# First expert's rows: tiles 0 and 1 fetched back from memory, the other six gathered by 0/1 products

## The chip, the cores and the metric

The kernel runs on one core of a Trainium2 chip. The time is device microseconds of one execution; before the change the median of three runs is 958.38 us (955.35 to 960.75). The engines are PE (TensorE: PE the products, PEld the weight loads), DVE (VectorE), ACT (ScalarE), POOL (GpSimd) and SP (SyncE, which only issues DMAs here).

## The reference

One decoder layer over 1024 positions of width 1024, in f32: a hybrid token mixer, a cross-attention into 256 memory tokens, and a mixture of 16 experts of which each token takes 2. The part that matters:

```python
xa = memory_cross_attention(x, mem, xa_wq[l], xa_wk[l], xa_wv[l], xa_wo[l])
x = layer_norm(DEEPNORM_ALPHA * x + xa, ln_xa_g[l], ln_xa_b[l])
ffn = grouped_moe(x, router_w, router_bias, expert_w_gate[l], expert_w_up[l], expert_w_down[l])
x = layer_norm(DEEPNORM_ALPHA * x + ffn, ln_moe_g[l], ln_moe_b[l])
```

`grouped_moe` takes the router's logits of x, a sigmoid, the best of 4 groups, the best 2 experts of it, and sums the two experts' outputs by weight.

## The kernel before, in words

The program is a row of blocks (`project`, `prepare`, `attend`, `cross_attend`, `experts`, `overflow`). In a block each engine has its own instruction list, written out by hand in the order in which it runs; semaphores join the lists. At the end of a block all engines meet at a barrier. The change lies wholly in `cross_attend`.

Positions stand in 8 tiles of 128. `cross_attend` walks over the tiles (t = 0 to 7) in one software pipeline. For a tile, PE makes queries, scores, values and output products (`outputs`, into the accumulator `x_acc`). DVE adds the residual and takes the statistics (`residual`), POOL turns the variance into 1/sigma (`ln_rs`, L1788 and L1789), DVE normalizes (`norm`, which signals `x2_made`). PE transposes the normalized tile (`turn_x2`, into `x_tps`), ACT copies it out (`copy_x2`, L1535), PE multiplies it with the router's weights (`logits`, L1414), ACT takes the exponential (`neg_exp`, L1539).

Slots are given out in three batches: tiles 0 to 3, 4 and 5, 6 and 7. Per batch DVE ranks the experts (`rank_experts`) and chooses two (`choose`, which makes `selected_b`); PE counts, with 0/1 products against a triangle and ones, how many tokens before have the same expert (`place`, L1426 and L1429); DVE makes of the counts the number of each token's row in a table (`number`, L1665 to L1678), of which every expert has 176 rows ("slots").

A token's row then goes two ways.

* To memory: POOL scatters it with two indirect DMAs per tile (`scatter`, L1770) into `slot_rows` in HBM, zeroed long before. When all 16 scatters have landed, SP in the next block loads 176 rows for each expert (`x_rows`).
* To the first expert alone, without memory: `number` also makes a 0/1 matrix per tile (`in_first_expert`, 128 tokens x 176 slots, L1671), and `first_rows` (L1456) multiplies each 128-column slice of the tile with it. Eight such products of 176 columns per tile add up over the 8 tiles in four PSUM banks (`first_ps`); ACT copies the four to `xgT` (L1586), the transposed input of the first expert. `first_rows` of tile 0 opens the accumulation.

The block's end is thus: `logits` of tile 7, ACT's exponential, DVE's `rank_experts(2)` and `choose(2)`, PE's `place(2)`, DVE's `number(2)`, then side by side PE's last `first_rows` and ACT's copies, and POOL's scatters of tiles 6 and 7; then the barrier, and `experts` begins with the first expert's gate and up products (L2016).

POOL's list in the last steps is: 1/sigma of tile 6, the two scatters of tile 0, 1/sigma of tile 7, the scatters of tiles 1 to 7.

Of the kernel before, what the change touches and what calls it, by code (L numbers as in the profile page):

```python
# [15 lines left out]
P = 128  # L16
S, D = 1024, 1024
NT = S // P
KD = D // P
# [1212 lines left out]
def cross_attend(nc, k):  # L1232
# [70 lines left out]
    dve_chain, pool_chain = k.sem("chain6"), k.sem("pool_chain6")  # L1303
    flat = "p j c -> p (j c)"
    BATCHES = [(0, 4), (4, 6), (6, 8)]
    with nc.psum_tensor("x_tps", [P, 2, 512], f32) as tps, nc.psum_tensor("x_qps", [P, 512], f32) as qps, \
            nc.psum_tensor("x_sps", [P, 2, 512], f32) as sps, nc.psum_tensor("x_ops", [P, 512], f32) as ops, \
            nc.psum_tensor("x_acc", [P, 2, 512], f32) as acc, nc.Block(no_gpsimd_drain=True) as block:
# [4 lines left out]
        @block.sync  # L1313
        def _(sp):
            sp.wait_ge(q_lo, KD)
            for s in range(XH):
                sp.dma_start(rawo[:, s, :], A["xa_wo"][s * P:(s + 1) * P, :]).then_inc(o_loaded, 16)
            sp.dma_start(rw[:], A["router_w"].rearrange("(s p) e -> p s e", p=P)).then_inc(rw_loaded, 16)
            sp.dma_start(rb[:], over(A["router_bias"], [P, NE])).then_inc(loaded, 16)
            sp.wait_ge(v_sum, 2)  # L1320
            sp.dma_start(g[:], over(A["ln_xa_g"], [P, D])).then_inc(loaded, 16)
            sp.dma_start(b[:], over(A["ln_xa_b"], [P, D])).then_inc(loaded, 16)

            sp.wait_ge(w_lo, XH)
            sp.dma_start(paired(k.e_dn[:]), A["w_dn"][0].rearrange("s p n -> p s n")).then_inc(k.dn_loaded, 16)
            sp.dma_start(k.g3[:], over(A["ln_moe_g"], [P, D])).then_inc(k.gains_loaded, 16)
            sp.dma_start(k.b3[:], over(A["ln_moe_b"], [P, D])).then_inc(k.gains_loaded, 16)
            sp.wait_ge(q_sum, NT)
            for e in range(2):
                sp.dma_start(paired(k.e_gu[:, e]), A["w_gu"][e].rearrange("s p n -> p s n")).then_inc(k.gu_loaded[e], 16)  # L1330

        @block.tensor
        def _(pe):
# [99 lines left out]
            def outputs(t, heads=range(XH)):  # L1433
                pe.wait_ge(o_lo, t + 1)
                if t == 0:
                    pe.wait_ge(w_lo, XH)
                    pe.wait_ge(v_taken, 2)
                if t:
                    pe.wait_ge(taken, t)
                for s in heads:  # L1440
                    for j in range(2):
                        o, c = acc[:, j, :], slice(512 * j, 512 * j + 512)
                        pe.matmul(o, ohi[:, s, :], k.xwo_hi[:, s, c], start=(s == 0), stop=False)
                        pe.matmul(o, ohi[:, s, :], k.xwo_lo[:, s, c], start=False, stop=False)
                        last = pe.matmul(o, olo[:, s, :], k.xwo_hi[:, s, c], start=False, stop=(s == XH - 1))
                if heads[-1] == XH - 1:
                    last.then_inc(summed, 1)

            def first_rows(t, chunks):
                pe.wait_ge(first_made, t + 1)  # L1450
                for s in chunks:
                    if t == 0 and s == 4:
                        pe.wait_ge(o_lo, NT)
                    if t == 0 and s == 6:
                        pe.wait_ge(taken, NT)
                    last = pe.matmul(first_ps[s // 2][:, (s % 2) * CAP:(s % 2 + 1) * CAP], x1[:, t, s * P:(s + 1) * P], in_first[:, t, :],  # L1456
                                     start=(t == 0 and s % 2 == 0), stop=(t == NT - 1 and s % 2 == 1))
                    if t == NT - 1 and s % 2:
                        last.then_inc(first_sum, 1)

            def memory_values(m, parts=range(KD)):
                pe.wait_ge(k.wv_loaded, 16 * KD)
# [7 lines left out]
            for t in range(NT):  # L1470
                queries(t, range(4))
                if t:
                    turn_probs(t - 1)
                queries(t, range(4, KD))
                if t:
                    values(t - 1)
                if t == 0:
                    memory_values(1, range(0, 1))
                turn_queries(t)
                if t == 0:  # L1480
                    memory_values(1, range(1, 2))
                elif t < 3:
                    turn(t + 1)
                else:
                    turn_x2(t - 3)
                scores(t)
                if t >= 3:
                    logits(t - 3)
                if t == 0 or 3 <= t < NT - 1:
                    turn(t + 1)  # L1490
                if t == 0:
                    memory_values(1, range(2, KD))
                if t:
                    outputs(t - 1, range(XH if t < NT - 1 else XH - 1))
            turn_probs(NT - 1)
            outputs(NT - 2, range(XH - 1, XH))
            turn_x2(NT - 3)
            values(NT - 1)
            place(0)
            logits(NT - 3)  # L1500
            outputs(NT - 1)
            turn_x2(NT - 2)
            first_rows(0, range(0, 4))
            logits(NT - 2)
            first_rows(0, range(4, KD))
            first_rows(1, range(KD))
            first_rows(2, range(0, 4))
            place(1)
            first_rows(2, range(4, KD))
            turn_x2(NT - 1)  # L1510
            first_rows(3, range(KD))
            logits(NT - 1)
            first_rows(4, range(KD))
            first_rows(5, range(0, 4))
            place(2)
            first_rows(5, range(4, KD))
            first_rows(6, range(KD))
            first_rows(7, range(0, 4))
            pe.wait_ge(ov_made, 1)
# [69 lines left out]
        def _(dve):  # L1589
# [70 lines left out]
            def number(n):  # L1660
# [6 lines left out]
                link(dve.tensor_tensor(val[:, t, :], val[:, t, :], fits[:, t, :], ALU.mult))  # L1667
                if n == 0:
                    dve.wait_ge(consts_made, 6)
                for u in range(lo, hi):  # L1670
                    dve.tensor_scalar(in_first[:, u, :], first_ids[:], val[:, u, 0:1], None, ALU.is_equal).then_inc(first_made, 1)  # L1671
                dve.tensor_reduce(code[:, t, 0], val[:, t, :], AX.X, ALU.max)
                link(dve.tensor_reduce(code[:, t, 1], val[:, t, :], AX.X, ALU.add))
# [28 lines left out]
            for t in range(NT + 1):  # L1702
# [15 lines left out]
                if t < NT:  # L1718
                    dve.wait_ge(exps, XH * (t + 1))
                    link(dve.reciprocal(rinv[:], rsum[:]))  # L1720
                    dve.tensor_tensor(prob[:], prob[:], over(rinv[:, :, None], [P, XH, MEM]), ALU.mult).then_inc(scaled, 1)
                if t >= 2:
                    norm(t - 2)
                if t == 0:
                    take_values(1)
# [3 lines left out]
                        dve.wait_ge(w_hi, s + 1)  # L1729
                        dve.tensor_tensor(k.xwo_lo[:, s, :], rawo[:, s, :], k.xwo_hi[:, s, :].bitcast(f32), ALU.subtract).then_inc(w_lo, 1)  # L1730
                if t == NT:
                    number(0)
                    rank_experts(1)
                if t:
                    residual(t - 1)
# [17 lines left out]
        def _(pool):  # L1753
# [29 lines left out]
            pool.tensor_tensor(mix_rs[:], mix_mv[:, 1:2], half[:], ALU.pow).then_inc(mix_rstd, 1)  # L1783
            for t in range(NT):
                if t == NT - 1:
                    scatter(0, [0])
                pool.wait_ge(var_ready, t + 1)
                link(pool.tensor_scalar(mv[:, t % 2, 1:2], mv[:, t % 2, 1:2], EPS, None, ALU.add))  # L1788
                pool.tensor_tensor(rs[:, t % 2:t % 2 + 1], mv[:, t % 2, 1:2], half[:], ALU.pow).then_inc(rstd_ready, 1)  # L1789
            scatter(0, [1, 2, 3])  # L1790
            scatter(1, [4, 5])
            scatter(2, [6, 7])

# [9 lines left out]
def paired(w):  # L1803

    return w.rearrange("p (s t) n -> p s (t n)", t=2)
# [697 lines left out]
```

## Time and profile before

| | us |
|---|---|
| median of three runs | 958.38 (955.35 to 960.75) |
| the profiled execution | 959.69 |
| its span in the profile | 957.8 |
| `cross_attend`, from POOL's last 1/sigma to the end | about 659 to 687.6 |
| PE busy, DVE busy, ACT busy, POOL busy | 925.9, 612.2, 351.3, 204.8 |

A timeline row gives the start and the length in us, the engine, the line, the operation, output<-inputs and how many instructions were merged; in brackets stands how long the engine had been idle before it and what ended that. One f32 product is two MATMUL records, so `first_rows` of a whole tile is 16 records; a transpose is one. Matmuls overlap, so what a group costs is the distance from its start to the next group's start.

### The profile page before, as it was taken

The page shows a single profiled execution, that of the slowest core. Times are in us where ns is not written, and L with a number is a line of the kernel's source. Part 1 is how long each engine was busy: PE and PEld are TensorE (multiplying, and loading weights), DVE is VectorE, ACT ScalarE, POOL GpSimd, SP SyncE. Part 2 cuts the span into 40 slices and gives each one's busy share as a digit, 9 for nine tenths or more (in the row PEclk, how much of TensorE's full clock was granted, in tenths as well). Part 3 has the DMA queues.
Part 4 walks back from the last instruction along what each step waited for, and adds up shares of the span by engine and source line. Part 5 has one row for each costly group of instructions (what it writes and reads, how often), then busy time and mean ns, then how long its engine had stood idle before and what let it go on. Part 6 is the DMA issues. An engine that isn't in the chain of part 4 may idle for free. (4 is left out here: it accounts for less than half of the span.)

```text
span 957.8 us, 15521 instructions
## 1 busy us (share of the span) xinstructions
PE 925.9 (97%) x5595; PEld 793.6 (83%) x5595; DVE 612.2 (64%) x1326; ACT 351.3 (37%) x737; POOL 204.8 (21%) x267
## 2 busy tenths in 40 slices
PE   7999999999999999999999999999699999999995
PEld 6899888787768888888867888889698989898984
DVE  6744341488677776645675454487445588888876
ACT  6133031354575555400024333431133244444442
POOL 0013100121161120012220000004200144444444
PEclk9999999999999999999999999999799999999998
DMA  9122001000699600710105000044678888989972
GB/s 309 69 89 88 1 18 50 1 1 1 216 414 411 243 23 13 255 64 1 67 32 207 6 1 1 1 176 166 229 265 300 292 311 306 332 326 337 338 273 100
DMA packets 54993, 151.64 MB, mean 158 GB/s; under 512 B 8720, under 2 KB 16144, under 8 KB 54928
## 3 DMA queue, kind: packets, MB, share of 16 engines
q1 hardware_dynamic: 47632, 133.82, 39.0%
q0 software_dynamic: 7296, 16.95, 4.7%
q8 instruction: 41, 0.67, 0.3%
q14 instruction: 24, 0.20, 0.1%
HBM read 107.62 MB, written 52.03 MB: 167 GB/s over the span
## 5 line engine op out<-in xcount | busy, mean ns | idle before, releaser
L2016 PE MATMUL h_ps<-xgT,e_gate_up 128*128 128x176 f32 x1024 | 157.1, 315 | 2.6 <-DVEq L2167 2.6
L2016 PEld LDWEIGHTS h_ps<-xgT,e_gate_up 128*128 128x128 f32 x1024 | 155.6, 192 | 4.4 <-issue 2.9
L270 PE MATMUL unit_ps<-whi,xhi 128*128 128x512 f32 (+1 forms) x256 | 98.1, 383 | 6.1 <-DVE wlo L308 6.1
L272 PE MATMUL unit_ps<-whi,xlo 128*128 128x512 f32 (+1 forms) x256 | 97.8, 382 | 0.0
L271 PE MATMUL unit_ps<-wlo,xhi 128*128 128x512 f32 (+1 forms) x256 | 97.7, 382 | 0.0
L270 PEld LDWEIGHTS unit_ps<-whi,xhi 128*128 128x128 f32 x256 | 48.6, 190 | 13.7 <-DVE xlo L352 6.1
L271 PEld LDWEIGHTS unit_ps<-wlo,xhi 128*128 128x128 f32 x256 | 48.6, 190 | 7.7
L272 PEld LDWEIGHTS unit_ps<-whi,xlo 128*128 128x128 f32 x256 | 48.5, 189 | 7.7
L2205 DVE SCALAR_TENSOR_TENSOR z<-y_ps,slot_weight,x_rows 128x512 f32<-128x512 f32 (+1 forms) x48 | 34.9, 750 | 23.9 <-PE y_ps L2029 23.5
L2119 ACT ACTIVATE ln_junk<-z,z_neg_mean 128x1024 f32<-128x1024 f32 (+1 forms) x24 | 27.6, 1149 | 45.5 <-issue 22.5
L1046 PE MATMUL t_ps<-constants,prob 128*128 128x128 f32 x288 | 41.2, 279 | 0.6 <-DVE prob_T L1194 0.4
L1063 PEld LDWEIGHTS o_ps<-prob_T,mla_v 128*64 128x64 f32 x576 | 30.8, 136 | 12.9 <-DVE prob_T L1194 8.9
L1063 PE MATMUL o_ps<-prob_T,mla_v 128*64 128x128 f32 x576 | 38.5, 278 | 3.0 <-DVE prob_T L1194 2.4
L2130 DVE TENSOR_TENSOR e_dn_lo<-e_down_raw,e_dn_hi 128x512 fp32r<-128x512 f32 x64 | 39.8, 678 | 0.8 <-ACT e_dn_hi L2092 0.8
L1194 DVE COPY prob_T<-t_ps 128x512 f32<-128x512 f32 (+3 forms) x48 | 29.7, 619 | 14.0 <-PE t_ps L1046 13.9
L1116 ACT ACTIVATE prob_T<-t_ps 128x128 f32<-128x128 f32 (+3 forms) x48 | 20.9, 436 | 47.1 <-PE t_ps L1046 47.1
L2092 ACT ACTIVATE e_dn_hi<-e_down_raw 128x512 fp32r<-128x512 f32 x64 | 35.1, 627 | 6.5 <-DVE ln_tmp L2175 4.6
L1046 PEld LDWEIGHTS t_ps<-constants,prob 128*128 128x128 f32 x288 | 31.4, 141 | 6.9 <-issue 5.4
L2146 DVE SCALAR_TENSOR_TENSOR ln_out<-ln_tmp,z_rstd,ln_b 128x1024 f32<-128x1024 f32 (+1 forms) x24 | 30.7, 1278 | 9.7 <-POOL z_rstd L1964 9.7
L862 ACT ACTIVATE mixT_hi<-s_ps 128x1024 fp32r<-128x1024 f32 x8 | 8.2, 1028 | 69.7 <-DVE s_ps L882 68.4
L1185 DVE TENSOR_REDUCE neg_max<-s_ps 128x1 f32<-128x640 f32 (+3 forms) x32 | 32.8, 1025 | 1.2
L1788 POOL TENSOR_SCALAR ln_mv<-ln_mv 128x1 f32<-128x1 f32 x8 | 1.8, 230 | 146.8 <-DVE ln_mv L1609 146.8
(379 smaller groups left out, 2223.9 us busy)
## 6 DMA issues: line engine op xcount, KB each, us to landing
e_gate_up<-w_gu SPq DMA_DIRECT2D x16, 2048.0 KB
e_down_raw<-w_dn SPq DMA_DIRECT2D x16, 1024.0 KB, 5.2
slot_rows<-zeros SPq DMA_DIRECT2D x22, 522.0 KB, 6.2
slot_sums<-zeros SPq DMA_DIRECT2D x22, 512.0 KB, 6.3
x_rows<-slot_rows SPq DMA_DIRECT2D x16, 522.0 KB, 6.0
slot_sums<-z SPq DMA_DIRECT2D x16, 512.0 KB, 6.4
wraw<-w_in SPq DMA_DIRECT2D x24, 256.0 KB, 4.5
xraw<-xT SPq DMA_DIRECT2D x16, 256.0 KB, 5.0
```

Of the source, the lines that this page charges most:

```text
L270: pe.matmul(o, hi, whi[:, s, 0:w], start=(s == 0), stop=False)
L271: pe.matmul(o, hi, wlo[:, s, 0:w], start=False, stop=False)
L272: last = pe.matmul(o, lo, whi[:, s, 0:w], start=False, stop=(s == KD - 1))
L1046: last = pe.transpose(tps[:, j, m * P:(m + 1) * P], prob[:, u % 2, j, m * P:(m + 1) * P], ident)
L1063: last = pe.matmul(ops[r, i % 2, (h // 2) * P:(h // 2 + 1) * P], k.v[:, m, h * MV:(h + 1) * MV], src, start=(m == 0), stop=(m == i))
L1185: dve.tensor_reduce(nmx[:, u % 2, 0:1], s[:, 0:(i + 1) * P], AX.X, ALU.max, negate=True).then_inc(max_ready, 1)
L1194: dve.tensor_copy(probT[:, v % 2, 0, 0:(z - a) * P], tps[:, 0, 0:(z - a) * P]).then_inc(pT_copied, 1)
L2016: end = pe.matmul(hps[:, m, gu * CAP:(gu + 1) * CAP], gate_up[:, b, s, w], xT[:, s, :], start=(s == 0), stop=(s == KD - 1))
L2092: act.activation(dn_hi[:, b, s, :], dn_raw[:, s, :], ACT.Copy).then_inc(dn_hi_done, 1)
L2130: dve.tensor_tensor(dn_lo[:, b, s, :], dn_raw[:, s, :], dn_hi[:, b, s, :].bitcast(f32), ALU.subtract).then_inc(dn_lo_done, 1)
L2146: dve.scalar_tensor_tensor(o[c][:], tmp[c][:], rs[r, c:c + 1], b_[r, :], ALU.mult, ALU.add).then_inc(out_made, 1)
L2205: dve.scalar_tensor_tensor(z[c][:, 512 * j:512 * j + 512], sums, wgt[r, b, c:c + 1], rest, ALU.mult, ALU.add, accum_out=out)\
```

## The change

Tiles 0 and 1 no longer go through 0/1 products. Their rows are scattered first, SP loads the first expert's 176 slots back from `slot_rows` (at this time they hold rows of these two tiles, or zeros) into a new tile `early`, 128 and 48 rows, and PE adds their transposes to the same four PSUM banks by products with the identity (`fetched_rows`: 8 products with 128 columns and 8 with 48). For this `place(0)` and `number(0)` move ahead into the last tile's step, POOL scatters both tiles before 1/sigma of tile 7, SP waits for the four scatters and for the last output products (`early` lies on `xwo_lo`, which they read), and POOL's later scatters wait until the load has landed. `first_rows(2)` now opens the accumulation. The line numbers of the new kernel are 6 to 13 higher here.

```diff
+    FETCHED = 2
+    early = at("first_rows_early", 153, [P, 2, D])
@@ sync
+            sp.wait_ge(summed, NT)
+            sp.wait_ge(k.rows_scattered, 16 * 2 * FETCHED)
+            sp.dma_start(early[:, 0, :], k.xs_dram[0:P, 0:D]).then_inc(o_loaded, 16)
+            sp.dma_start(early[0:CAP - P, 1, :], k.xs_dram[P:CAP, 0:D]).then_inc(o_loaded, 16)
@@ tensor
             def first_rows(t, chunks):
-                pe.wait_ge(first_made, t + 1)
+                pe.wait_ge(first_made, t + 1 - FETCHED)
...
+            def fetched_rows():
+                pe.wait_ge(o_loaded, 16 * XH + 32)
+                for s in range(KD):
+                    o, c = first_ps[s // 2], (s % 2) * CAP
+                    w = slice(s * P, (s + 1) * P)
+                    pe.matmul(o[:, c:c + P], early[:, 0, w], ident, start=False, stop=False)
+                    pe.matmul(o[:, c + P:c + CAP], early[0:CAP - P, 1, w], ident[0:CAP - P, 0:CAP - P], start=False, stop=False)
@@ after the loop over the tiles
+            place(0)
             turn_probs(NT - 1)
             outputs(NT - 2, range(XH - 1, XH))
             turn_x2(NT - 3)
             values(NT - 1)
-            place(0)
             logits(NT - 3)
             outputs(NT - 1)
             turn_x2(NT - 2)
-            first_rows(0, range(0, 4))
+            first_rows(2, range(0, 4))
             logits(NT - 2)
-            first_rows(0, range(4, KD))
-            first_rows(1, range(KD))
-            first_rows(2, range(0, 4))
+            first_rows(2, range(4, KD))
+            first_rows(3, range(KD))
             place(1)
-            first_rows(2, range(4, KD))
             turn_x2(NT - 1)
-            first_rows(3, range(KD))
+            fetched_rows()
             logits(NT - 1)
             first_rows(4, range(KD))
-            first_rows(5, range(0, 4))
+            first_rows(5, range(KD))
             place(2)
-            first_rows(5, range(4, KD))
             first_rows(6, range(KD))
@@ vector
-                for u in range(lo, hi):
+                for u in range(max(lo, FETCHED), hi):
...
-                if t >= 2:
+                if t == NT - 1:
+                    norm(t - 2)
+                    number(0)
+                elif t >= 2:
                     norm(t - 2)
...
                 if t == NT:
-                    number(0)
                     rank_experts(1)
@@ gpsimd
                 if t == NT - 1:
-                    scatter(0, [0])
+                    scatter(0, range(FETCHED))
...
-            scatter(0, [1, 2, 3])
+            pool.wait_ge(o_loaded, 16 * XH + 32)
+            scatter(0, range(FETCHED, 4))
```

On DVE, from `norm(5)` to `rank_experts(1)` of the kernel before (`x_72` is the tile `x1`, L1616 the end of a `norm`, L1604 to L1609 `residual(6)`, L1707 the low half for the last output products, L1665 to L1678 `number(0)`):

```order
 L1616 SCALAR_TENSOR_TENSOR x_72<-ln_tmp,ln_rs,ln_b 128x1024
 L1604 SCALAR_TENSOR_TENSOR x_72<-x_72,x_acc 128x1024
...
 L1609 BN_AGGR ln_mv<-ln_st 128x2
 L1707 TENSOR_TENSOR xoT_lo<-x_ops,xoT_hi 128x512
 L1615 SCALAR_TENSOR_TENSOR ln_tmp<-x_72,ln_mv,ln_g 128x1024
 L1616 SCALAR_TENSOR_TENSOR x_72<-ln_tmp,ln_rs,ln_b 128x1024
 L1665 SCALAR_TENSOR_TENSOR fits<-x_sps,selected 128x64
...
 L1671 TENSOR_SCALAR in_first_expert<-first_expert_ids,slot_val 128x176 x4
...
 L1678 TENSOR_SCALAR x_72<-slots 128x4
 L1634 TENSOR_SCALAR neg_exp<-neg_exp 128x32
```

and the same stretch of the kernel after:

```order
 L1627 SCALAR_TENSOR_TENSOR x_72<-ln_tmp,ln_rs,ln_b 128x1024
 L1676 SCALAR_TENSOR_TENSOR fits<-x_sps,selected 128x64
...
 L1682 TENSOR_SCALAR in_first_expert<-first_expert_ids,slot_val 128x176 x2
...
 L1689 TENSOR_SCALAR x_72<-slots 128x4
 L1615 SCALAR_TENSOR_TENSOR x_72<-x_72,x_acc 128x1024
...
 L1620 BN_AGGR ln_mv<-ln_st 128x2
 L1718 TENSOR_TENSOR xoT_lo<-x_ops,xoT_hi 128x512
 L1626 SCALAR_TENSOR_TENSOR ln_tmp<-x_72,ln_mv,ln_g 128x1024
 L1627 SCALAR_TENSOR_TENSOR x_72<-ln_tmp,ln_rs,ln_b 128x1024
 L1645 TENSOR_SCALAR neg_exp<-neg_exp 128x32
```

`number(0)` now stands ahead of `residual(6)`, the low half and `norm(6)`, with two 0/1 matrices in place of four.

On PE, from the second `place` to the third, before (`x_sps`, `x_ops` and `x_acc` are the banks of the first expert's rows, L1403 the transposes of tile 7, L1414 its logits):

```order
 L1426 MATMUL x_acc<-selected_b,up_to 128x32
...
 L1403 MATMUL x_tps<-constants,x_72 128x128 x8
 L1456 MATMUL x_sps<-in_first_expert,x_72 128x176 x4
...
 L1414 MATMUL x_qps<-router_w,x2T 128x16 x8
 L1456 MATMUL x_sps<-in_first_expert,x_72 128x176 x4
...
 L1426 MATMUL x_acc<-selected_b,up_to 128x32
```

and after:

```order
 L1432 MATMUL x_acc<-selected_b,up_to 128x32
...
 L1409 MATMUL x_tps<-constants,x_72 128x128 x8
 L1472 MATMUL x_sps<-constants,first_rows_early 128x128
 L1473 MATMUL x_sps<-constants,first_rows_early 128x48
...
 L1420 MATMUL x_qps<-router_w,x2T 128x16 x8
 L1462 MATMUL x_sps<-in_first_expert,x_72 128x176 x4
...
 L1432 MATMUL x_acc<-selected_b,up_to 128x32
```

Between the transposes of tile 7 and its logits stand now the 16 products on the fetched rows, where `first_rows(3)` stood; all of `first_rows(5)` is ahead of the third `place`, where half of it was.

## Rows read from the trace of the kernel before

**Rows 1.** The page: busy time of the engines, share of the span, instructions.

```profile
PE 925.9 (97%) x5595; PEld 793.6 (83%) x5595; DVE 612.2 (64%) x1326; ACT 351.3 (37%) x737; POOL 204.8 (21%) x267
```

**Rows 2.** Timeline of PE, 645 to 690 us: start, length, engine, line, operation.

```profile
645.16 1.95 PE L1393 MATMUL x_ops<-xprobT,xv 128*128 128x128 f32 x16
646.95 0.19 PE L1426 MATMUL x_sps<-selected_b,up_to 128*128 128x64 bf16 x1
...
648.85 0.48 PE L1443 MATMUL x_acc<-xwo_hi,xoT_hi 128*128 128x512 f32 x1
...
664.62 1.04 PE L1403 MATMUL x_tps<-constants,x 128*128 128x128 f32 x8
665.50 1.36 PE L1456 MATMUL x_sps<-in_first_expert,x 128*128 128x176 f32 x8
...
667.89 1.85 PE L1414 MATMUL x_qps<-router_w,x2T 128*128 128x16 f32 x16
669.59 1.44 PE L1456 MATMUL x_sps<-in_first_expert,x 128*128 128x176 f32 x8
...
678.19 0.21 PE L1426 MATMUL x_acc<-selected_b,up_to 128*128 128x32 bf16 x1 [4.77 <-DVE selected_b L1652]
...
678.42 1.52 PE L1456 MATMUL x_ops<-in_first_expert,x 128*128 128x176 f32 x4
...
689.68 10.52 PE L2016 MATMUL h_ps<-xgT,e_gate_up 128*128 128x176 f32 x58 [2.63 <-DVEq L2167]
```

**Rows 3.** Timeline of ACT: tile 7's exponential and the last copy to `xgT`.

```profile
673.95 0.18 ACT L1539 ACTIVATE neg_exp<-x_qps 128x16 f32<-128x16 f32 x1 [7.23 <-remote]
...
687.09 0.46 ACT L1586 ACTIVATE xgT<-x_acc 128x352 f32<-128x352 f32 x1
```

**Rows 4.** Timeline of POOL: scatters and 1/sigma.

```profile
647.69 0.57 POOL L1789 TENSOR_TENSOR ln_rs<-ln_mv,ln_half 128x1 f32<-128x1 f32 x1
654.76 1.24 POOL L1770 DMA_INDIRECT slot_rows<-x,slots  x1 [6.50 <-DVE x L1678]
...
672.76 0.96 POOL L1770 DMA_INDIRECT slot_rows<-x,slots  x1 [0.30 <-issue]
681.92 1.17 POOL L1770 DMA_INDIRECT slot_rows<-x,slots  x1 [8.20 <-DVE x L1678]
...
685.93 0.96 POOL L1770 DMA_INDIRECT slot_rows<-x,slots  x1 [0.30 <-issue]
```

**Rows 5.** Timeline of DVE, 644 to 681 us.

```profile
644.51 1.22 DVE L1604 SCALAR_TENSOR_TENSOR x<-x,x_acc 128x1024 f32<-128x1024 f32 x1 [0.33 <-PE x_acc L1445]
...
647.78 0.69 DVE L1707 TENSOR_TENSOR xoT_lo<-x_ops,xoT_hi 128x512 fp32r<-128x512 f32 x1 [0.49 <-ACT xoT_hi L1560]
...
651.02 0.22 DVE L1665 SCALAR_TENSOR_TENSOR fits<-x_sps,selected 128x64 f32<-128x64 f32 x1
...
651.67 0.97 DVE L1671 TENSOR_SCALAR in_first_expert<-first_expert_ids,slot_val 128x176 f32<-128x176 f32 x4
...
653.69 0.17 DVE L1634 TENSOR_SCALAR neg_exp<-neg_exp 128x32 f32<-128x32 f32 x1
...
662.73 1.28 DVE L1616 SCALAR_TENSOR_TENSOR x<-ln_tmp,ln_rs,ln_b 128x1024 f32<-128x1024 f32 x1
```

**Rows 6.** DMA to and from `slot_rows`: of 640 to 700 us, then of all.

```profile
x_rows<-slot_rows SPq DMA_DIRECT2D x2, 522.0 KB, 5.3
...
DMA to landing us min/median/max: 2.8/6.1/8.3
```

**Rows 7.** Windows of 2 us: length, busy PE, PEld, DVE, ACT, POOL, PEclk, DMA share, GB/s.

```profile
658.00:660.00 2.00, 2.00 (x16) 2.00 (x16) 1.90 (x11) 0.18 (x1) 0.58 (x2) 1.00 0.65 267
660.00:662.00 2.00, 2.00 (x15) 2.00 (x14) 1.79 (x9) 0.00 (x0) 1.46 (x3) 1.00 0.01 4
...
680.00:682.00 2.00, 2.00 (x8) 2.00 (x8) 1.76 (x12) 0.00 (x0) 0.08 (x1) 0.50 0.00 0
...
690.00:692.00 2.00, 2.00 (x8) 2.00 (x8) 1.72 (x2) 0.00 (x0) 0.00 (x0) 0.50 0.37 40
```

More of the change, by code:

```diff
@@ L1449, in first_rows @@
             def first_rows(t, chunks):
-                pe.wait_ge(first_made, t + 1)
+                pe.wait_ge(first_made, t + 1 - FETCHED)
                 for s in chunks:
-                    if t == 0 and s == 4:
+                    if t == FETCHED and s == 4:
                         pe.wait_ge(o_lo, NT)
-                    if t == 0 and s == 6:
+                    if t == FETCHED and s == 6:
                         pe.wait_ge(taken, NT)
                     last = pe.matmul(first_ps[s // 2][:, (s % 2) * CAP:(s % 2 + 1) * CAP], x1[:, t, s * P:(s + 1) * P], in_first[:, t, :],
-                                     start=(t == 0 and s % 2 == 0), stop=(t == NT - 1 and s % 2 == 1))
+                                     start=(t == FETCHED and s % 2 == 0), stop=(t == NT - 1 and s % 2 == 1))
                     if t == NT - 1 and s % 2:
                         last.then_inc(first_sum, 1)
+            def fetched_rows():
[5 more added lines that the diff above has]
+                    pe.matmul(o[:, c + P:c + CAP], early[0:CAP - P, 1, w], ident[0:CAP - P, 0:CAP - P], start=False, stop=False)
             def memory_values(m, parts=range(KD)):
```

## The prediction, made before the changed kernel ran

> **What bounds the kernel now.** The page has PE busy 97% of the span [rows 1], so the first question is where PE stands still near the change. The timeline of PE shows two gaps: 4.77 us before the third `place` and 2.63 us before the first expert's products at 689.68 [rows 2]. I then read backwards from 689.68 through the timelines of the engines that meet at the barrier. ACT's last copy ends at 687.55 (687.09 + 0.46) [rows 3]; POOL's last scatter leaves the engine at 686.89 (685.93 + 0.96) [rows 4]. So PE's chain (products of tiles 5 to 7, ACT's copies) sets the barrier, and POOL's chain is only 0.66 us behind. Both start from one event: `selected_b` of the last batch, which hangs on tile 7's exponential at 673.95 [rows 3]. That one is odd: the logits' products run from 667.89 and the next group starts at 669.59, yet ACT gets its signal 4.2 us after that, "ended by remote" [rows 2, 3]. I call this the late signal; nothing in the rows says whether each execution has it. What the change is worth is thus read from three things: when `logits` of tile 7 ends, what PE still has to do after the third `place`, and what POOL has to do.
>
> **DVE.** `number(0)` goes from 651.02 to 653.69, 2.67 us. Two of its four 0/1 matrices (0.97 us for four) go: 2.67 - 0.48 = 2.2 us [rows 5]. It now starts where `norm(5)` ends, 644.18 (644.51 - 0.33), so `residual(6)` comes at 646.4, 1.9 later. The low half stood behind 0.49 us of idle time; it now starts at 647.78 - 0.49 + 1.9 = 649.2 and ends at 649.9 [rows 5]. PE's output products of tile 7, which began at 648.85 [rows 2], wait for it until 649.9: +1.05. POOL's 1/sigma of tile 6 (done at 648.26 [rows 4]) moves to 650.2, `norm(6)` ends at 652.9. There `number(0)` stood, so ranking of tiles 4 and 5 starts at 652.9 instead of 653.69, and all behind it, to the end of `norm(7)`, gains 0.75: 664.01 (662.73 + 1.28) becomes 663.25 [rows 5]. The 0.82 us of idle time that goes (0.33 + 0.49) and the 0.48 us of matrices pay for the waits that come.
>
> **PE up to tile 7's logits.** Of 648.85 to 664.62 one tile of `first_rows` falls out (0 and 1 go, 3 comes in). A tile costs 667.89 - 665.50 = 2.39 us [rows 2]. So the transposes of tile 7 can start at 649.9 + 15.77 - 2.39 = 663.3, just when `norm(7)` is done, and end at 664.2 (0.88 from 664.62 to 665.50). Then come the 16 products on fetched rows. The nearest rows: 16 records of 128 columns take 646.95 - 645.16 = 1.79 us, so the eight 128-column products cost 1.79. For the 48-column ones I have 16 records of 16 columns in 669.59 - 667.89 = 1.70 us from below and 1.79 from above; I take 1.75. Together 3.55 us: logits start at 667.75 against 667.89. PE's work shrinks by 4.78 - 3.55 = 1.2 us, but tile 7's logits gain 0.1 only, because the fetched products (3.55) stand where one tile (2.39) stood.
>
> **The round trip through memory.** This is the added wait. POOL could scatter from 646.4, but its list has 1/sigma of tile 6 first, so the first scatter starts at 650.4. Pitch: 1.24 + 0.30, then 0.96 + 0.30 [rows 4]: the fourth starts at 654.5. The scatter issued as second before, about 656.30 (654.76 + 1.54), had its data through by 660, since the DMA share falls from 0.65 to 0.01 there [rows 7]: 3.7 us at most. So the four have landed at 658.2, with a little backlog 658.5; the output products (`summed`) are done at 655.4, earlier. SP's load of 704 KB takes 5.3 us by the equal pair of `x_rows` loads [rows 6]: 663.8, against PE's wish at 664.2. It is hidden by 0.4 us. The ends are 2.8 us (nothing more to gain) and 8.3 us (PE waits 2.6 us) [rows 6]. Behind PE's wait stand the logits of tile 7, and for these everything waits; behind SP's nothing until the next block; behind POOL's wait the scatters of tiles 2 to 7. Eight of them take 8 x 1.26 = 10.1 us to 674; the next are due when `number(2)` is done, 681.9 [rows 4]. Cover of nearly 8 us, or 3.7 if the late signal were gone.
>
> The Trainium skill ("DMA: Bandwidth & Descriptors", section "Anatomy of one DMA — SWDGE (gpsimd) path") puts a DMA at about 2.0 us plus its bytes over 436 GB/s, most of the 2.0 being the confirmation of the last byte, heaviest with HBM as the target. An estimate by it is 3.2 us for a scatter and 3.65 us for the load, 6.9 us together against the 9.0 of my rows. Its bytes-and-constant view lets the load be hidden by 2 us more; the rows are taken from this kernel and decide. No sum changes.
>
> **The end of the block.** After the third `place` PE has two tiles instead of two and a half. At full rate that is 1.2 us less; PE is at half its clock there (granted 0.50 in 680 to 682 [rows 7], that is 1.2 GHz, after the 4.77 us gap), so the half tile is worth up to 2.4. ACT's last copy ends at 686.35 or before. But POOL's four scatters are not touched and end at 686.8: the barrier moves from ACT's 687.55 to POOL's, 0.7 us. That is the whole gain of the block; the rest of PE's saving becomes a longer gap before 689.68.
>
> **Sum.** -0.1 (logits) - 0.6 (barrier) = -0.7 us. The profiled execution of 959.69 (span 957.8) would be 959.0; the median shown, 958.38, lies 1.3 below it: 957.7 us. Nothing of `experts` changes: its loads of rows wait for the last scatter, as before.
>
> **Rivals.**
> *The late signal goes.* The change puts other instructions on PE around the logits. If the exponential follows them at once, both chains come 4.2 us earlier; the barrier is POOL's in any case. 957.7 - 4.2 = 953.5; PE then stands still some 5 to 6 us before `experts` rather than 2.63, which may prolong the half rate that the row at 690 shows (0.50 [rows 7]) and give 1 us back: 954.3. For it: one such signal in one profile, and runs that lie 5.4 us apart, as if some had it and some not. Against it: the conditions (scatters filling the DMA engines at that time, the same order logits, tile 4, tile 5) stay. The Trainium skill ("Runtime: NRT & Kernel Launch", "Instruction fetch mechanics") says that an engine fetches its code by its own DMA queue, the cost mostly hidden; if the late signal is a fetch behind scatters, the rule would not let it be seen, the 4.2 us would. No row here tells.
> *The load is late* (the slower side). Its place is PE's wait before tile 7's logits, its price one us for each us that the load takes over 5.7 (664.2 - 658.5), and it decides from there on. With 8.3 us: +2.6 on both chains, 957.7 + 2.6 = 960.3; with some work at half rate after the wait 961.5. For it: the margin is 0.4 us, built on three estimated shifts; the median of all transfers on `slot_rows` is 6.1. Against it: POOL waits, so no other transfer runs beside the load.
> *The clock.* PE's gap before `experts` grows from 2.63 to above 3 us, and the half rate that the row at 690 shows [rows 7] lasts 3 to 4 us longer than now; half of that is lost, +1.7: 959.4.
> *The change's saving counts where I say it does not:* POOL does not hold the barrier, and PE's 1.2 to 2.4 us count in full: 956.2. Against it: 686.89 stands in the row.
>
> **How the numbers follow.** Forecast 957.7: 0.42; signal gone, 954.3: 0.23; load late, 960.3: 0.15; clock, 959.4: 0.10; PE in full, 956.2: 0.10. 0.5% is 4.8 us, which is about what a measurement here can tell from none: faster is below 953.6, slower above 963.2. The first is reached by the better half of the signal case and by a lucky median: 0.16. The second needs a late load at 8.3 us and half rate and an unlucky median: 0.05. The rest, 0.79, is no change. Range: 953.2 (signal gone, nothing given back) to 961.3 (late load with half rate); by itself the forecast has 955.5 to 960.0, from the spread of the runs.
>
> **What would show it.** Right: PE idle about 1 us before tile 7's output products; the fetched products in 3.4 to 3.7 us with no idle time ahead; logits of tile 7 at 667.7 and POOL's last scatter ending after ACT's last copy. Wrong: idle time of PE before the fetched products (the load), an exponential right behind the logits (the signal), a first expert's product more than 1.5 us earlier with the exponential where it was, or half rate for more than 4 us after the first expert starts.

## The result, and the profile after

The changed kernel is a little slower: 961.58 us median (959.86 to 963.78, 15 runs) against 959.98 for the kernel before, run beside it; the ratio over all runs is 1.0029 (95% interval 1.0020 to 1.0039), which is 2.8 us, while the two medians lie 1.6 us apart. A second comparison later gave 1.0034 (1.0021 to 1.0048). I call this some 3 us more; I had forecast 0.7 us less, 957.7 us, and a range up to 961.3. The profiled execution took 963.24 us, its span is 961.4 against 957.8, and the page shows where to look: PE is busy 6.1 us longer with the same number of instructions [rows 1], while DVE and POOL are busy within 1 us as long as before.

```profile
PE 932.0 (97%) x5595; PEld 796.2 (83%) x5595; DVE 611.4 (64%) x1324; ACT 350.9 (36%) x737; POOL 204.3 (21%) x267
```

PE's timeline over the stretch, to be read against [rows 2]:

```profile
650.08 0.50 PE L1449 MATMUL x_acc<-xwo_hi,xoT_hi 128*128 128x512 f32 x1 [0.88 <-DVE xoT_lo L1718]
...
657.28 1.03 PE L1409 MATMUL x_tps<-constants,x 128*128 128x128 f32 x8
...
665.14 1.09 PE L1409 MATMUL x_tps<-constants,x 128*128 128x128 f32 x8
666.11 0.49 PE L1472 MATMUL x_sps<-constants,first_rows_early 128*128 128x128 f32 x2
666.53 0.42 PE L1473 MATMUL x_sps<-constants,first_rows_early 48*128 48x48 f32 x2
666.88 0.49 PE L1472 MATMUL x_sps<-constants,first_rows_early 128*128 128x128 f32 x2
...
672.79 3.59 PE L1420 MATMUL x_qps<-router_w,x2T 128*128 128x16 f32 x16
676.22 2.69 PE L1462 MATMUL x_sps<-in_first_expert,x 128*128 128x176 f32 x8
...
683.77 0.18 PE L1432 MATMUL x_acc<-selected_b,up_to 128*128 128x32 bf16 x1
...
692.83 7.40 PE L2030 MATMUL h_ps<-xgT,e_gate_up 128*128 128x176 f32 x48 [2.42 <-DVEq L2181]
```

The fetched products run from 666.11 to 672.79, 6.7 us where I had written 3.55, with no idle time ahead of them. One pair (a 128-row product and a 48-row product) takes 666.88 - 666.11 = 0.77 us. Then the logits take 3.43 us (before 1.70), and tiles 4 and 5 of `first_rows` 7.55 us (676.22 to 683.77) where two tiles at full rate take 4.78. The windows say why (columns as in [rows 7], the eighth is PEclk):

```profile
650.00:652.00 2.00, 1.92 (x6) 1.54 (x7) 1.52 (x3) 0.00 (x0) 1.49 (x2) 0.75 0.00 0
652.00:654.00 2.00, 2.00 (x6) 1.57 (x5) 1.86 (x5) 0.00 (x0) 1.70 (x2) 0.50 0.29 121
...
670.00:672.00 2.00, 2.00 (x11) 1.62 (x10) 0.00 (x0) 0.00 (x0) 1.46 (x2) 0.87 0.93 368
672.00:674.00 2.00, 2.00 (x10) 1.71 (x8) 0.00 (x0) 0.00 (x0) 1.63 (x2) 0.50 0.93 368
...
680.00:682.00 2.00, 2.00 (x10) 2.00 (x9) 1.38 (x8) 0.00 (x0) 0.00 (x0) 0.57 0.08 29
```

Towards the end of the fetched products the granted clock falls to 0.50 (1.2 of 2.4 GHz) and stays there to about 681.7; a shorter such stretch follows PE's wait of 0.88 us at 650.

ACT's and POOL's rows, to be read against [rows 3, 4]:

```profile
676.42 0.18 ACT L1550 ACTIVATE neg_exp<-x_qps 128x16 f32<-128x16 f32 x1 [9.13 <-issue]
...
690.45 0.46 ACT L1597 ACTIVATE xgT<-x_acc 128x352 f32<-128x352 f32 x1
```

```profile
687.09 1.18 POOL L1783 DMA_INDIRECT slot_rows<-x,slots  x1 [10.25 <-DVE x L1689]
...
691.11 0.96 POOL L1783 DMA_INDIRECT slot_rows<-x,slots  x1 [0.30 <-issue]
```

The late signal is gone: the exponential follows the end of the logits (676.22) by 0.20 us, where it was 4.36 us before. The books, before to after:

| | before | after | |
|---|---|---|---|
| transposes of tile 7 start | 664.62 | 665.14 | +0.5 |
| logits start | 667.89 | 672.79 | +4.9 |
| logits end (next group starts) | 669.59 | 676.22 | +6.6 |
| exponential | 673.95 | 676.42 | +2.5 |
| third `place` | 678.19 | 683.77 | +5.6 |
| ACT's last copy ends | 687.55 | 690.91 | +3.4 |
| first expert's products | 689.68 | 692.83 | +3.2 |

So the change lost 6.6 us, got 4.2 back by the prompt signal, lost 3.1 again because PE was still busy with tiles 4 and 5 when `selected_b` was ready (at 680.63 by DVE's row), got 2.2 back at the end (half a tile less after the third `place`, and full rate again) and 0.2 in the step to the first expert. Of the 3.6 us between the two spans, 0.2 stood already ahead of this stretch and 0.4 came behind it.

### The profile page after: what moved, and what is told of

It is laid out like the page before. It is cut to its first block and busy times, and to the rows that moved or that the text cites. A ratio compares the mean times of both kernels' runs of the same rounds, so it can differ in the third digit from the quotient of the medians.

```text
span 961.4 us, 15523 instructions
## 1 busy us (share of the span) xinstructions
PE 932.0 (97%) x5595; PEld 796.2 (83%) x5595; DVE 611.4 (64%) x1324; ACT 350.9 (36%) x737; POOL 204.3 (21%) x267
## 5 line engine op out<-in xcount | busy, mean ns | idle before, releaser
L272 PEld LDWEIGHTS unit_ps<-whi,xlo 128*128 128x128 f32 x256 | 48.3, 189 | 7.8
```

The source lines that it names most:

```text
L272: last = pe.matmul(o, lo, whi[:, s, 0:w], start=False, stop=(s == KD - 1))
```

## The experiments

My theory after this profile: the fetched products are dear because each product is followed by one with another number of weight rows (128, 48, 128, ...), and they pull the clock down behind them. The rivals that I set against it: the moved slots and scatters cost the time; the load or the gap at 650 does; or it is chance.

**The same bytes, other products.** Two kernels keep everything but the form of the fetched products. One puts the eight of 128 rows first:

```diff
-                for s in range(KD):
+                for b in range(2):
+                    for s in range(KD):
...   b == 0: the product with early[:, 0, w] and ident
...   b == 1: the product with early[0:CAP - P, 1, w] and ident[0:CAP - P, 0:CAP - P]
```

> The 16 products on the fetched rows take 6.7 us in the changed kernel where 3.55 were foreseen. Here the eight of 128 rows come first, then the eight of 48 rows. Theory A (PE pays for every change between weights of 128 rows and of 48 rows): one change in place of fifteen, so the 16 products take 3.4 to 4 us, tile 7's logits come 2.5 to 3 us earlier or more (less half rate), and the kernel is 3 to 5 us faster than the changed one, at or below the kernel before. Theory B (a 48-column or 48-row product is slow by itself): they still take over 6 us and the time stays.

The other keeps the order, loads 128 rows in place of 48 and multiplies all of them with the identity's first 48 columns:

```diff
-            sp.dma_start(early[0:CAP - P, 1, :], k.xs_dram[P:CAP, 0:D]).then_inc(o_loaded, 16)
+            sp.dma_start(early[:, 1, :], k.xs_dram[P:2 * P, 0:D]).then_inc(o_loaded, 16)
-                    pe.matmul(o[:, c + P:c + CAP], early[0:CAP - P, 1, w], ident[0:CAP - P, 0:CAP - P], start=False, stop=False)
+                    pe.matmul(o[:, c + P:c + CAP], early[:, 1, w], ident[:, 0:CAP - P], start=False, stop=False)
```

> As changed, in the alternating order, but the second product of each slice takes all 128 rows of the second block (identity columns 0 to 47), for which the load brings 1 MB in place of 704 KB. Theory A (change of row count): no change of rows is left, 16 products in 3.4 to 3.7 us although 128 and 48 columns still alternate; the load may land 0.7 us later and give some of it back. Theory B (48 columns are slow, or alternating columns): 6 us and more. Rival C (products are slow because of the loaded data or its memory): 6 us and more as well.

Measured on one chip: grouped 957.59, ratio to before 0.9971 (0.9957 to 0.9985); full rows 956.90, 0.9965 (0.9951 to 0.9979). Both lie below the kernel before, and, ratio against ratio, some 0.6% below the changed one, which did not run beside them. PE's timeline of the grouped kernel:

```profile
650.27 0.50 PE L1449 MATMUL x_acc<-xwo_hi,xoT_hi 128*128 128x512 f32 x1 [0.87 <-DVE xoT_lo L1721]
...
665.62 1.16 PE L1474 MATMUL x_sps<-constants,first_rows_early 128*128 128x128 f32 x8 [0.82 <-DMA first_rows_early<-slot_rows]
...
667.60 1.09 PE L1476 MATMUL x_sps<-constants,first_rows_early 48*128 48x48 f32 x8
...
669.51 2.96 PE L1420 MATMUL x_qps<-router_w,x2T 128*128 128x16 f32 x16
```

and of the one with full rows:

```profile
665.92 0.49 PE L1472 MATMUL x_sps<-constants,first_rows_early 128*128 128x128 f32 x2 [1.05 <-DMA first_rows_early<-slot_rows]
666.25 0.32 PE L1473 MATMUL x_sps<-constants,first_rows_early 128*128 128x48 f32 x2
666.41 0.45 PE L1472 MATMUL x_sps<-constants,first_rows_early 128*128 128x128 f32 x2
666.70 0.32 PE L1473 MATMUL x_sps<-constants,first_rows_early 128*128 128x48 f32 x2
666.85 0.45 PE L1472 MATMUL x_sps<-constants,first_rows_early 128*128 128x128 f32 x2
...
669.53 1.92 PE L1420 MATMUL x_qps<-router_w,x2T 128*128 128x16 f32 x16
```

Sixteen products take 3.89 us grouped (1.98 for those of 128 rows, 1.91 for those of 48) and 3.61 with full rows (0.44 a pair). Neither size is dear by itself: the alternation is. At full rate eight alternating pairs take 8 x 0.765 = 6.12 us; against 3.89 that is 2.2 us for 14 more changes, 0.16 us each. The clock is the second half: with full rows no half rate comes before 680, while in the grouped kernel it is there from about 670.2, and the logits take 2.8 us. The window 670 to 672 of the grouped kernel, then of the one with full rows:

```profile
670.00:672.00 2.00, 2.00 (x13) 2.00 (x12) 0.00 (x0) 0.00 (x0) 1.39 (x3) 0.56 0.91 365
```

```profile
670.00:672.00 2.00, 2.00 (x19) 2.00 (x19) 0.00 (x0) 0.00 (x0) 1.39 (x3) 1.00 0.93 370
```

Grouping takes the 0.16 us away, full rows take both. The half rate needs no alternation, then: the grouped kernel has it too. And being without it did not make full rows clearly faster: the intervals of the two overlap for the most part. Full rows lose again behind it: the counts of the third `place`, whose last products end at 677.09, reach DVE 1.5 us later (in the changed and the grouped kernel 0.04 us), PE then waits 2.41 us for the 0/1 matrices, and half rate follows.

```profile
678.59 0.19 DVE L1676 SCALAR_TENSOR_TENSOR fits<-x_acc,selected 128x32 f32<-128x32 f32 x1 [0.95 <-PE x_acc L1435]
```

One part of the gap between these kernels and the changed one has nothing to do with the edit. All three wait 0.87 to 0.88 us at 650, ahead of any fetched product, and only the changed one has half rate behind it. But the two others then wait for the load, so that its fetched products start only 0.5 and 0.2 us behind theirs (666.11 against 665.62 and 665.92).

The comparison once more, with five rounds each, on another chip:

> The changed kernel once more, on the same chip as the two below. Theory (the products on fetched rows with 48-row weights are dear and bring the half rate): 1.0 to 4.5 us above the kernel before, ratio 1.001 to 1.005; its profile has 0.7 to 0.8 us per pair of fetched products and half rate behind them. Rival (the 0.3% was one chip's or one day's scatter): ratio within 0.999 to 1.001.

> Edit: the second fetched product takes all 128 rows. Theory: 4 to 6 us below the changed kernel on the same chip, ratio to before 0.995 to 0.998. Rival (the first comparison was luck, since the same edit with number(0) placed later came out at 1.0019): ratio 0.999 to 1.002.

The changed kernel came to 961.54 (1.0034, interval 1.0021 to 1.0048), full rows to 956.73 (0.9980, 0.9970 to 0.9991): 4.8 us for one edit. Full rows against before was under the 0.5% that I call telling, but both its intervals lie below 1. The new profiles repeat the old ones: fetched products 7.1 us with half rate from about 671.1 in the changed kernel, 3.61 us at full rate with full rows. From DVE's reciprocal at about 640 (L1720 before) to the first expert's products it is 49.5 and 50.1 us in the two profiles of the kernel before, 52.4 and 51.9 in the changed one, 47.9 grouped, 48.3 and 48.3 with full rows. So 3.6 to 4.0 of the 4.8 us lie in this stretch.

**The slots alone.** The kernel before, with `place(0)` and `number(0)` moved into the last tile's step and nothing else:

```diff
+            place(0)
             turn_probs(NT - 1)
...
-            place(0)
@@ vector
+                if t == NT - 1:
+                    number(0)
...
-                    number(0)
                     rank_experts(1)
```

> The kernel before with one part of the change alone: the first batch's count and slots in the last tile's step, all eight tiles still by 0/1 products, tile 0 alone scattered ahead of the last 1/sigma. Theory 1 (the move of the slots costs by PE's gap of about 1 us before tile 7's output products, sometimes with half clock behind it): gap of 1.2 us there, and the time 0 to 2 us above the kernel before. Theory 2 (the move is free or a gain, since it takes DVE's idle time): ranking of tiles 4 and 5 starts earlier, and the time is equal or up to 1 us less.

959.87 (958.43 to 964.01), ratio 1.0017 (1.0005 to 1.0029), which is +1.6 us (0.5 to 2.8). Here all four 0/1 matrices are still made in DVE's step, so PE waits longer than in the changed kernel:

```profile
650.46 0.50 PE L1443 MATMUL x_acc<-xwo_hi,xoT_hi 128*128 128x512 f32 x1 [1.34 <-DVE xoT_lo L1707]
...
669.53 1.85 PE L1414 MATMUL x_qps<-router_w,x2T 128*128 128x16 f32 x16
671.23 0.99 PE L1456 MATMUL x_sps<-in_first_expert,x 128*128 128x176 f32 x5
```

The logits move from 667.89 to 669.53. That is a cost of the move, but no half rate follows in this profile. By its interval alone it could be most of the 3 us; but full rows and grouped have the same move and are faster than the kernel before, so it does not decide the sign.

**Taking the gap at 650 away.** The changed kernel, with `number(0)` where it was (in the step after the last tile, ahead of `norm(6)`):

```diff
-                if t == NT - 1:
-                    norm(t - 2)
+                if t == NT:
                     number(0)
-                elif t >= 2:
+                if t >= 2:
                     norm(t - 2)
```

> As changed, but DVE makes the first batch's slots after the low half of tile 7 instead of before the residual of tile 6. The changed kernel has PE idle 0.9 us ahead of tile 7's output products and then half clock from 651.0 to 654.4 us. Theory (the short wait costs the clock): no idle time there, granted clock 1.0 throughout 650 to 656, output products 5.5 us in place of 7.2, and the kernel 1 to 2.5 us faster than the changed one. Rival (the gap costs its 0.9 us and the load is what is late, so PE waits at the fetched rows): PE idle before the fetched rows and under 1 us faster.

I expected it faster, a miss: it was the slowest of all with several runs: 964.28, ratio 1.0046 (1.0029 to 1.0062). The gap at 650 was gone as I had said, and two others came: DVE's last `norm` is later, and the load is no sooner.

```profile
663.99 1.09 PE L1409 MATMUL x_tps<-constants,x 128*128 128x128 f32 x8 [1.46 <-DVE x L1627]
666.15 0.61 PE L1472 MATMUL x_sps<-constants,first_rows_early 128*128 128x128 f32 x2 [1.06 <-DMA first_rows_early<-slot_rows]
...
667.28 0.79 PE L1472 MATMUL x_sps<-constants,first_rows_early 128*128 128x128 f32 x2
668.00 0.66 PE L1473 MATMUL x_sps<-constants,first_rows_early 48*128 48x48 f32 x2
668.59 0.79 PE L1472 MATMUL x_sps<-constants,first_rows_early 128*128 128x128 f32 x2
...
676.47 3.59 PE L1420 MATMUL x_qps<-router_w,x2T 128*128 128x16 f32 x16
```

Behind the two waits the half rate is there from about 666.4, a pair takes 1.31 us, and the products 10.3 us. The same edit on top of full rows:

> The second product of full 128 rows (as in the faster variant) together with the first batch's slots made behind the low half of tile 7. Theory (the fetched products with changing row counts were what kept the clock at half from 666 to 683 us in the variant with the low half first, which was 3 us slower than the changed kernel): with full rows no half clock during the fetched products, logits of tile 7 done by 671.5 us as in the full-rows variant, and its time within 1 us of it (956.9). Rival (PE's wait of about 1 us for the load, with another 1.5 us before the transposes of tile 7, brings half clock by itself): half clock from about 666 us again and 2 to 5 us slower than the full-rows variant.

960.68 (955.22 to 963.31), 1.0019 (1.0005 to 1.0033), where full rows had 0.9965 and 0.9980: again a miss. Against the same order without full rows (1.0046, interval from 1.0029) it is the lower one, though the two intervals touch. The profile (span 958.0) has the two waits (1.47 and 1.22 us) and no half rate before 678.4, and does not show the loss; the runs go with their mean clock, 955.22 at 0.995 and 963.31 at 0.986. That executions differ in whether the half rate follows the two waits fits both numbers, but I have a profile of one alone, so it is not shown.

**The late signal.** The kernel before, profiled in another execution:

> The kernel before once more, for one thing: is the signal of tile 7's logits late in each execution (4.2 us between the products' end and ACT's exponential), or only in the profile shown? If it is a property of the kernel, it is there again and the span is 957 to 959; if it is chance, the exponential follows within 0.3 us of the products and the span is about 955.

960.33 us. The signal is late again: the logits start at 668.31 and the exponential runs at 674.97 [7.82 <-remote]. So it is in both profiles of this kernel, and in the one with only the slots moved (exponential 3.85 us after the logits' end): it is not one execution's chance. Then full rows with tile 0's scatters ahead of tile 6's 1/sigma, so that the load and the later scatters come earlier:

```diff
+                if t == NT - 2:
+                    scatter(0, [0])
...
-                    scatter(0, range(FETCHED))
+                    scatter(0, [1])
```

> Full 128 rows, and POOL scatters tile 0 already ahead of 1/sigma of tile 6, so that the fourth scatter and the load come about 2.5 us earlier. Theory (in the full-rows variant PE waits 1.05 us for the load and that stands on the path of tile 7's logits): idle time before the fetched products gone, logits 1 us earlier, and the kernel about 1 us faster than the full-rows variant (956.9), near 956. Rival (1/sigma of tile 6 comes later by what the scatters take, and DVE hands the loss on): transposes of tile 7 later by 0.5 us or more and no gain.

958.08, 0.9996 (0.9981 to 1.0012), where I expected 956: a miss. The wait for the load went (fetched products at 665.16, logits from 668.66 to 670.44), and none of it arrived, since ACT's row reads

```profile
673.97 0.18 ACT L1550 ACTIVATE neg_exp<-x_qps 128x16 f32<-128x16 f32 x1 [7.58 <-remote]
```

The later scatters ran from 663.0 instead of 666.7 here, and the late signal was back. The reverse test is the kernel before with POOL's scatters of tiles 1 to 7 held until the exponential of tile 7:

```diff
+            pool.wait_ge(neg_done, NT)
             scatter(0, [1, 2, 3])
```

> The kernel before, with POOL's scatters of tiles 1 to 7 held back until ACT has made tile 7's exponential. Theory (the signal of tile 7's logits is late because the scatters fill the DMA engines at that time, 667 to 676 us): the exponential follows the logits' products within 0.3 us, at about 670. Rival (it is late whatever DMA does, by PE's own queue): it is again at 674 to 675. The time will be longer, since twelve scatters then stand before the barrier; it tells nothing here.

964.19 us in one run. ACT's timeline:

```profile
669.90 0.18 ACT L1539 ACTIVATE neg_exp<-x_qps 128x16 f32<-128x16 f32 x1 [3.06 <-PE x_qps L1414]
690.80 0.82 ACT L1586 ACTIVATE xgT<-x_sps 128x352 f32<-128x352 f32 x2 [20.72 <-remote]
```

The exponential came 0.2 us after its products; but the scatters now ran from 670.89 to 688.50 without a pause, and PE's signals for the four finished banks (its last product starts at 681.53) all reached ACT at 690.8. The delay follows the scatters, not the logits. (One run, and its time tells nothing: twelve scatters then stand before the barrier.)

**Logits ahead of the fetched products.** Last, a version to use this: full rows, the logits moved ahead so that they end when the scatters have just begun.

```diff
             turn_x2(NT - 1)
-            fetched_rows()
+            first_rows(4, range(0, 4))
             logits(NT - 1)
-            first_rows(4, range(KD))
-            first_rows(5, range(KD))
+            fetched_rows()
+            first_rows(4, range(4, KD))
+            first_rows(5, range(0, 4))
             place(2)
+            first_rows(5, range(4, KD))
```

> Edit: all 128 rows, and the fetched products moved behind the logits of tile 7, with half of first_rows(4) ahead of the logits in their place; half of first_rows(5) is again behind the third place. Theory (the fetched products are dear where they stand, because tile 7's logits wait for them, and the signal of the logits is prompt as long as the scatters have only just begun): logits end at about 667.7 instead of 671.3, PE does not wait for the load any more, the exponential follows within 1 us, the third place comes at 673 to 675, POOL's last scatter ends at 681 to 683, and the first expert's products start 3 to 5 us sooner than with full rows alone: 952 to 954, ratio 0.992 to 0.995. Rival (the signal comes when it comes, near 672.5, because the scatters hold it): exponential at 671.5 to 673, nothing gained beyond full rows: 956 to 957.5, ratio 0.996 to 0.998.

956.29 (955.79 to 957.47), ratio 0.9974 (0.9965 to 0.9983), beside 956.73 for full rows on the same chip: the fastest median, though not told apart from full rows. The step that I expected came in full (exponential at 667.08, third `place` at 672.93, before any other kernel here), and was then taken back by the next signal. DVE's row for the counts of `place`, whose products had ended by 673.14:

```profile
677.37 0.19 DVE L1678 SCALAR_TENSOR_TENSOR fits<-x_acc,selected 128x32 f32<-128x32 f32 x1 [4.95 <-remote]
```

```profile
672.00:674.00 2.00, 1.98 (x20) 1.81 (x19) 0.38 (x2) 0.00 (x0) 1.41 (x2) 1.00 0.95 372
674.00:676.00 2.00, 0.85 (x4) 0.51 (x3) 0.00 (x0) 0.00 (x0) 1.49 (x2) 1.00 0.99 388
676.00:678.00 2.00, 0.06 (x1) 0.00 (x0) 0.56 (x4) 0.00 (x0) 0.00 (x0) 1.00 0.98 386
678.00:680.00 2.00, 1.72 (x6) 1.72 (x7) 1.79 (x11) 0.00 (x0) 0.00 (x0) 0.56 0.44 175
```

The signal is 4.2 us late and comes 1.6 us after the last scatter of the row has left POOL (675.79). I had expected 952 to 954 and POOL's last scatter at 681 to 683; it ended at 685.29. The rival of that expectation named the wrong signal, but its time (956 to 957.5) was the right one.

## Why the prediction was wrong

*What bounds the kernel* was read half right. PE's chain to ACT's last copy is the end, and the late signal is real. POOL was further from setting the end than the 0.66 us, though. From the end of ACT's last copy to the first expert's products it is 1.8 to 2.1 us in all 13 profiles (before 2.13, after 1.92), whatever POOL does; POOL's last scatter ended 0.75 to 5.7 us before them (before 2.79, after 0.76). In the changed kernel POOL ended 1.16 us after ACT, and still the distance from ACT did not grow. So the two ends may not be compared as they stand, and the step "the barrier moves from ACT's 687.55 to POOL's, 0.7 us" falls. (There was not much room left: POOL's next instruction, at 692.38, follows its last scatter after 0.30 us, the gap that stands between any two scatters.) The end of the block was also worth more than 0.7 us: from the third `place` to ACT's last copy the kernel after takes 7.1 us against 9.4.

*DVE.* Right in kind: PE waited 0.88 us for the low half (1.05 foreseen). What I priced at nothing was the clock behind this wait: half rate from about 651 to 654.4, so that the output products ended at 657.28 and not at 655.4, and the transposes of tile 7 started at 665.14, not 663.3. That was not bound to happen: five other profiles with a wait of 0.87 to 0.91 us at the same place have no half rate behind it.

*The fetched products* are the step that failed: the term "Together 3.55 us", with 6.7 measured, and full rate taken for granted behind it. I took the price of a product from rows in which equal products follow each other, and the change makes them alternate. The forms were right: grouped they take 3.89, with full rows 3.61, within 0.35 of my sum. The alternation costs 2.2 us, the fall of the clock within them the other 0.6, and what the clock did behind them was more than both: 1.7 us in the logits, and 2.8 in tiles 4 and 5 (7.55 against 4.78), where I had counted on full rate.

*The round trip.* The load was hidden, by a margin near nothing, as foreseen (PE's row at 666.11 has no wait), but only because PE was 1.8 us later than I had it. The four scatters took longer and the load less: SP issued it at 661.4, 5.7 us after the fourth scatter's start at 655.7 and not 4.0, and it landed 4.7 us later and not 5.3. With PE on time the load is late, by 0.82 us grouped and 1.05 and 1.24 us in the two profiles of full rows (which load 1 MB). The estimate for the pair from the Trainium skill's figures ("DMA: Bandwidth & Descriptors", "Anatomy of one DMA — SWDGE (gpsimd) path"), 6.9 us, is further off than my 9.0; 10.4 were measured from the fourth scatter's start to the landing, with the scatters queued behind each other. (That section is on DMAs issued by GpSimd, and the load is issued by SP.)

*The rivals.* The late signal did go, to which I had given 0.23, and by itself, 4.2 us at the exponential, it would have made the kernel faster. "The clock" had the right cause in the wrong place: before the first expert I expected the half rate, and it came 20 us earlier and cost more. "Load late" was not what happened. None of them held the alternation. The time lies in the band of no change, to which I gave 0.79, but just above the end of my range, and near it only by two large errors that partly cancel (6.6 us lost at the logits, 4.2 got back by the signal): that it came so near is luck. Two rivals that act together in different directions (signal gone, clock down) were never added up.

What is shown: the form of the fetched products decides the sign (two edits, one repeated on another chip), and the alternation of 128 and 48 weight rows makes the sixteen products 2.2 us longer. Shown as a cost that does not decide it: the moved slots, 1.6 us by themselves. Not settled: how PE's signals are held up, and what starts the half rate behind the fetched products. It follows them grouped and alternating and not with full rows, but whether they alone bring it or the gap at 650 has a part is open; the kernel without that gap had other gaps.

## What to carry to other kernels

Price a product by rows in which its neighbours are the new neighbours: equal products in a row say nothing of a list in which the number of weight rows changes each time. If the sizes differ, fill the smaller one up or group by size, and where PE is the bound, look behind a cheap or broken stretch for what the clock does to the work that follows, which can cost more than the stretch (here 4.5 us behind an excess of 3.1). When a wait ended by "remote" goes, look at the next signal from the same engine before counting the gain.

## What the runs showed that was not expected

In these profiles PE's signals are late while indirect scatters fill the DMA engines and PE is at full rate. From the start of the next group on PE to the receiver's instruction: 4.36 us before (4.96 in its second profile), 3.85 with the slots moved, 3.53 with tile 0's scatters first, 1.2 and 1.05 with full rows, 4.2 for the counts in the last kernel, and about 9 with the scatters held. In the same order the scatters had started 9.1 (9.1), 10.9, 7.4, 4.6, 4.6, 7.3 and 11 us before. Where they had run for 1.1 us it was 0.19. The late ones above 3 us all came near the end of the row of scatters, from 0.1 us before to 2.3 us after POOL's last one had ended.

At half rate the signal of the logits was prompt each time, 0.20 us: in the changed kernel 9.4 and 9.9 us into the scatters, grouped 5.9 us, and 13.0 us in the kernel with the low half first. That these kernels escaped the delay because their clock was down is what the numbers suggest; no experiment tested it alone. One number warns against the simple form of it: with the scatters held, the granted clock was at 0.50 from about 686 while PE stood idle, and the signals still did not come before 690.8. So a clock that falls after the products does not free them.

DVE's signals are held up as well as ACT's (4.2 us for the counts in the last kernel, 1.5 with full rows). The Trainium skill ("Runtime: NRT & Kernel Launch", "Instruction fetch mechanics") has instructions fetched by their own DMA queue, and PE does show a few idle times ended by "issue" in such stretches (0.36 and 0.81 us in the last kernel). But the profile shows no packet at all on an instruction queue while the signal was out in three of the late cases (671 to 675.5 with the slots moved, 673 to 677.8 in the last kernel, 680 to 691 with the scatters held), which speaks against a fetch as the cause.

A wait of about 1 us on PE is sometimes followed by some 3 us of half rate and sometimes not, and the same wait in the same place can do either. The wait of 0.87 to 0.91 us for the low half at 650, with the same list of products ahead of it, is followed by it in both profiles of the changed kernel and in none of the five others that have it (grouped, full rows twice, tile 0's scatters first, and the last kernel). A profile of one execution therefore does not show what such a wait costs.
